# Attention outputs by features: values held in TensorE on two column halves, probabilities divided on GpSimd before their transpose

## The reference, cut to what matters

```
g = sigmoid(gates)
o_a = g[0] * softmax(q kc) vc  +  g[1] * softmax(q k_slc) v_slc  +  g[2] * softmax(q k_win) v_win
e = exp(s - m);  p = e / (sum(e) + exp(sink - m));  o_b = p v_swa
merged = sigmoid(ga) * (o_a @ w_branch_a) + sigmoid(gb) * (o_b @ w_branch_b)
h = h + merged @ w_out
```

```
x = x + concatenate([o_mla, o_dsa, o_ret]) @ w_out
x = x + square(relu(rmsnorm(x) @ w_ff1)) @ w_ff2
```

## Time and profile before

| | us |
|---|---|
| median of 3 runs | 1260.78 |
| lowest, highest | 1260.34, 1265.6 |
| time of the profiled execution | 1260.99 |
| its span in the trace | 1259.2 |

### The profile page before, as it was taken

The page is one execution under the profiler, slowest core; times in us unless marked ns, Lnnn a source line. Parts: engine busy times, 40 slices in busy tenths (PEclk is TensorE's granted clock), DMA queues, the critical chain, the costliest instruction groups (busy, mean ns, idle before and its releaser), DMA issues. The chain is left out here.

```text
span 1259.2 us, 21554 instructions
## 1 busy us (share of the span) xinstructions
PE 1228.6 (98%) x8764; PEld 1131.6 (90%) x8764; DVE 791.7 (63%) x1095; ACT 609.6 (48%) x831; POOL 66.4 (5%) x58
## 2 busy tenths in 40 slices
PE   8999999999999999999999899999999989999997
PEld 7999999989998999999999789999999978999996
DVE  4665556657866655555799655555458977654554
ACT  5444345355536443435755554444465464544343
POOL 0000000200000000000530000000004200000000
PEclk9999999999999999999999999999999999999999
DMA  9576565455335565556465056655644734566550
GB/s 286 176 227 193 175 184 149 129 159 169 134 119 199 179 192 197 173 193 185 151 126 168 28 174 203 197 175 193 187 140 119 159 101 151 174 195 192 176 198 33
DMA packets 200915, 209.62 MB, mean 166 GB/s; under 512 B 58136, under 2 KB 177552, under 8 KB 200848
## 3 DMA queue, kind: packets, MB, share of 16 engines
q1 hardware_dynamic: 200400, 208.21, 53.8%
q10 hardware_dynamic: 448, 0.46, 0.2%
HBM read 207.61 MB, written 1.05 MB: 166 GB/s over the span
## 5 line engine op out<-in xcount | busy, mean ns | idle before, releaser
L1366 DVE TENSOR_TENSOR w_lo<-raw,w_hi 128x2048 fp32r<-128x2048 f32 (+2 forms) x192 | 432.9, 2258 | 270.5 <-ACT w_hi L1014 269.9
L1014 ACT ACTIVATE w_hi<-raw 128x2048 fp32r<-128x2048 f32 (+2 forms) x192 | 359.4, 1876 | 246.3 <-PE bank L1890 214.8
L1890 PE MATMUL bank<-n_hi,w_hi 128*128 128x256 f32 (+1 forms) x1600 | 455.4, 285 | 1.5 <-DVE w_lo L1366 1.5
L1890 PE MATMUL bank<-n_hi,w_lo 128*128 128x256 f32 (+1 forms) x1600 | 452.8, 283 | 0.0
L1890 PE MATMUL bank<-n_lo,w_hi 128*128 128x256 f32 (+1 forms) x1600 | 452.7, 283 | 0.0
L1890 PEld LDWEIGHTS bank<-n_hi,w_hi 128*128 128x128 f32 (+1 forms) x1600 | 305.3, 191 | 5.6 <-DVE w_lo L1366 1.7
L1890 PEld LDWEIGHTS bank<-n_lo,w_hi 128*128 128x128 f32 (+1 forms) x1600 | 305.3, 191 | 2.1 <-issue 0.2
L1890 PEld LDWEIGHTS bank<-n_hi,w_lo 128*128 128x128 f32 (+1 forms) x1600 | 305.3, 191 | 0.0
L1890 PE MATMUL bank<-w_hi,hid_hi 128*128 128x512 f32 x440 | 172.7, 392 | 1.3 <-DVE hid_lo L1439 1.1
L1890 PE MATMUL bank<-w_lo,hid_hi 128*128 128x512 f32 x440 | 171.8, 391 | 0.0
L1890 PE MATMUL bank<-w_hi,hid_lo 128*128 128x512 f32 x440 | 171.4, 389 | 0.0
(11 more groups left out here) (268 smaller groups left out, 1485.5 us busy)
## 6 DMA issues: line engine op xcount, KB each, us to landing
raw<-in_w_ff_dram SPq DMA_DIRECT2D x64, 1024.0 KB, 5.3
raw<-in_w_in_dram SPq DMA_DIRECT2D x31, 1024.0 KB, 5.4
raw<-in_ffn_down_dram SPq DMA_DIRECT2D x22, 1024.0 KB, 4.9
raw<-in_ffn_up_dram SPq DMA_DIRECT2D x21, 1024.0 KB, 5.4
raw<-in_ffn_gate_dram SPq DMA_DIRECT2D x20, 1024.0 KB, 5.4
raw<-in_w_out_dram SPq DMA_DIRECT2D x12, 1024.0 KB, 5.1
raw<-in_w_in_dram SPq DMA_DIRECT2D x12, 256.0 KB, 4.0
raw<-in_w_uq_dram SPq DMA_DIRECT2D x24, 128.0 KB, 4.0
```

Source lines behind the costliest of these rows:

```text
L1014: nc.scalar.activation(wh(s)[:, c0:n], raw[:, s % RING, c0:n], ACT.Copy).then_inc(hi_ready, 1)
L1366: V.tensor_tensor(wl(s)[:, c0:n], raw[:, s % RING, c0:n], wh(s)[:, c0:n].bitcast(f32), ALU.subtract).then_inc(lo_ready, 1)
L1890: mm = MM(out, stat(k, a), mov(k, b), start=(first and k == 0 and n == 0), stop=(last and k == K - 1 and n == 2), skip_group_check=True)
```

## The change

Five parts:

1. **Values stationary, column halves.** `pv` holds 64 columns of values and streams the transposed probabilities of all the heads of a group (256 or 512 columns; in mla 128, since each head has its own values). The upper group writes partitions 0 to 63 of the bank, the lower group 64 to 127, so two matmuls with different columns of the array stand next to each other. The output has features on partitions.
2. **Division ahead of the turn.** A softmax sum now belongs to a column of the output, so it is divided out earlier: a new step `n` stands between `s` and `t`. VectorE makes the factor `pcoef` (reciprocal, in layer 0 times the gate), and GpSimd multiplies the round's two `probs` buffers by it in place. `t` waits on `normed` in place of `exp_done`.
3. **Branches summed in the bank.** `slc`, `win` and the compressed branch of a tile add up in one PSUM bank (step `o` `nsa`); the compressed probabilities are multiplied by their factor on VectorE (in `cs`).
4. **No output transposes** but for retention (4 in place of 16 per layer); step `o` is a copy to hi on ScalarE and a subtraction to lo on VectorE.
5. **Order.** Layer 0 starts with `swa` and ends with `win`; branch b comes before branch a. Layers 1 and 2 have a new order, in which the first quarter of `wout` (the rows of dsa and ret) stands between the mla rounds. `probsT` gets two more buffers.

```diff
-    S += gate[2] + [("cmpt", "v")] + scores[4] + weighted[2] + turned[3]
+    S += gate[2] + [("cmpt", "v")] + scores[4] + normed[3] + weighted[2] + turned[3]
...
+        scores, normed, turned, weighted = in_rounds(l, [("dsa", 0), ("dsa", 1), ("mla", 0), ("mla", 1)])
+        S += scores[0] + scores[1] + [("ukv", l)] + normed[0] + turned[0] + scores[2] + [("ukvv", l)] + normed[1] + turned[1]
+        S += [("rety", l)] + scores[3] + weighted[0] + normed[2] + weighted[1] + [("mixt", l)] + turned[2] + scores[4] + normed[3]
+        S += [("wout", l, 0)] + turned[3] + weighted[2] + normed[4] + turned[4] + weighted[3] + weighted[4]
+        S += [("wout", l, n) for n in range(1, 4)]
...
+                if st[0] == "n":
...
+                    pool.wait_ge(coef_ready, CO[(l, a, t, next(r for r in rounds(a, t) if g in r))] + 1)
+                    by = pcoef[:, RSLOT[a], t, hs].unsqueeze(2).to_broadcast([P, nh, nk])
+                    p = probs[:, q % 4, 0:nh * nk].rearrange("p (h k) -> p h k", h=nh)
+                    nc.gpsimd.tensor_tensor(p, p, by, ALU.mult).then_inc(normed, 1)
...
+                elif kind == "n":
...
+                    dve.wait_ge(exp_done, ATT[(l, a, t, r[1])] + 1)
...
+                    ins = V.reciprocal(c, sums)
+                    if a in GATE:
+                        link(ins)
+                        dve.wait_ge(*free_count(("toks", 0)))
+                        ins = V.tensor_tensor(c, c, of(gates[:, t, 8 * GATE[a]:8 * GATE[a] + 8]), ALU.mult)
+                    ins.then_inc(coef_ready, 1)
...
                 elif kind == "t":
                     q = ATT[st[1:]]
-                    pe.wait_ge(exp_done, q + 1)
+                    pe.wait_ge(normed, NRM[st[1:]] + 1)
...
-                    for i, h in enumerate(heads):
-                        for blk in range(t + 1):
-                            c = (i * (t + 1) + blk) * P
-                            mm = MM(acc[o % 2][:, h * HD:h * HD + HD], probsT[:, n % 2, c:c + P], values(a, h, blk),
-                                    start=(blk == 0), stop=(blk == t))
+                    for blk in range(t + 1):
+                        for i in range(nh if a == "mla" else 1):
+                            for rows_, heads, pT in sides:
+                                c0, n = column_of(a, heads[i]), (1 if a == "mla" else nh)
+                                mm = MM(ob[rows_, c0:c0 + n * P].rearrange("p (i c) -> p i c", c=P), values(a, heads[i], blk), pT[:, i:i + n, blk, :],
+                                        start=(first and blk == 0 and i == 0), stop=(blk == t), skip_group_check=True)
...
+                elif kind == "o":
+                    ob, ks, tok = output_blocks(st)
+                    act.wait_ge(pv_done, ON[st[1:]][1])
...
+                    nc.scalar.activation(on_hi[:, ks, tok], ob, ACT.Copy).then_inc(ot_hi, 1)
```

More of the change, by code:

```diff
@@ L138, in schedule @@
[L138 to L141, removed]
+    S += scores[0] + [("proj", 0, "nq1"), ("rope", 0, "sq1"), ("cmpt", "k")] + scores[1] + normed[0] + [("rope", 0, "nq1")] + turned[0]
@@ L142, in schedule @@
+    S += gate[6] + [("ct", 1)] + scores[8] + normed[7] + weighted[6] + [("cv", 0), ("o", 0, "nsa", 0)] + turned[7]
+    S += gate[7] + [("sigmoid",)] + normed[8] + weighted[7] + turned[8] + [("cv", 1)] + weighted[8] + [("o", 0, "nsa", 1), ("branch",)]
     S += [("wout", 0, n) for n in range(4)]
@@ L155, in schedule @@
               ("topk", l, 1, 0, 4), ("topk", l, 1, 4, 8), ("proj", l, "rg"), ("uq", l, 1),
[L156 to L165, removed]
+              ("retv", l), ("rope", l, "uq"), ("uq", l, 2), ("retn", l)]
+        scores, normed, turned, weighted = in_rounds(l, [("dsa", 0), ("dsa", 1), ("mla", 0), ("mla", 1)])
[3 more added lines that the diff above has]
+        S += [("wout", l, n) for n in range(1, 4)]
         S += [("split", 3 + 2 * l), ("root", 3 + 2 * l), ("stat", 3 + 2 * l), ("ffn2", l)]
@@ L1335, in _ @@
                 elif kind == "wout" and st[2] < 2:
[L1336 removed]
+                    ahead(SL[st], 1 if st[1] and st[2] == 0 else 2)
         @block.vector
@@ new lines, in _ @@
+                    V.tensor_tensor(on_lo[:, ks, tok], ob, on_hi[:, ks, tok].bitcast(f32), ALU.subtract).then_inc(o_free, 1)
+                elif kind == "n":
+                    _, l, a, t, g = st
+                    r = next(r for r in rounds(a, t) if g in r)
+                    if g != r[0]:
+                        continue
+                    dve.wait_ge(exp_done, ATT[(l, a, t, r[1])] + 1)
+                    hs = sorted(groups(a, t)[r[0]] + groups(a, t)[r[1]])
+                    if a in GATE:
+                        of = lambda x: x.rearrange("p (g j) -> p g j", g=2)[:, :, hs[0]:hs[len(hs) // 2 - 1] + 1]
+                    else:
+                        of = lambda x: x[:, hs[0]:hs[-1] + 1]
+                    c = of(pcoef[:, RSLOT[a], t, :])
+                    sums = of(rsum[:, RSLOT[a], t, :])
+                    if a == "swa":
+                        link(V.tensor_tensor(c, sums, of(esink[:, t, :]), ALU.add))
+                        sums = c
+                    ins = V.reciprocal(c, sums)
+                    if a in GATE:
+                        link(ins)
+                        dve.wait_ge(*free_count(("toks", 0)))
+                        ins = V.tensor_tensor(c, c, of(gates[:, t, 8 * GATE[a]:8 * GATE[a] + 8]), ALU.mult)
+                    ins.then_inc(coef_ready, 1)
+                elif kind == "wout" and st[1] and st[2] == 0:
+                    ahead(SL[st], 1)
@@ L2223, in _ @@
                     _, l, a, t, g = st
-                    heads, n, o = groups(a, t)[g], PVN[st[1:]], ON[st[1:4]][0]
+                    r = next(r for r in rounds(a, t) if g in r)
+                    if g != r[0]:
+                        continue
+                    key = output_of(l, a, t)
+                    ob, begun = acc[ON[key][0] % 2], key in opened
                     if g == 0:
```

312 lines of the change are left out of this document (143 added, 169 removed).

## The result

The changed kernel takes 1302.73 us (median of four runs), the kernel before, timed beside it, 1263.19; the ratio is 1.0306, with a 95% interval of 1.026 to 1.0352. The prediction said 1302. That median counts one run of 1796.31 us, far above the others, which the ratio leaves out: the other three took 1299.95, 1300.54 and 1304.92 us. The profiled execution took 1299.95 us, its span is 1298.2, and its mean granted clock 0.982.

What follows compares the result with a forecast made beforehand. PE, busy 98% of the span, was taken to bound the kernel. From 1261.0 us, 21 for layer 0's stalls, 10 for layers 1 and 2 and 10 for clock falls gave 1302; range 1277 to 1322.

Steps and rivals of the forecast that it cites:

- What bounds: PE, busy 98% of the span before; afterwards idle before turns, some 30 us in layer 0, 25 in layers 1 and 2.
- The chain of a round: Layer 0, scores through maxima, factor and two GpSimd products to the turn: gate at S + 6.3 us instead of S + 3.70.
- the stall is half as long: Rival: GpSimd's product with a repeated factor is quicker than the rotation's rows, or signals are shorter; 1275 us, chance 0.10.
- Layer 0: Attention's nine turns wait for GpSimd's product, whose factor stands behind the next round's maxima: 21 us longer in sum.
- Layers 1 and 2: PE waits 14.5 us per layer, against old waits, values and transposes saved: 5 us longer each, 10 for both.
- The clock: Gaps of about 2.5 us before turns drop the granted clock to half: nine falls at 1.1 us, 10 us; bounds 0 and 32.
- Part 1: Times-values on PE: column halves run side by side, halving 33.1 us of matmuls, so 16.5 us saved.
- Part 4: Output transposes on PE: 40 of 48 go, 4 us, with a 1.6 us wait before the branches' second half; 5.6 together.
- Ports: GpSimd products meeting a VectorE split would cost 1.6 us more; none expected, nothing added. Rival that they meet: 1320 to 1330, chance 0.04.
- 1239 if nothing new waited: Whole kernel: 1261 less 22 us of PE's own work, should the change bring no new waits.
- The saving of 22 us: PE's own work saved by the values matmuls (16.5 us) and output transposes with their wait (5.6 us).
- the faster case: Rival: the turn does not wait, normalized probabilities being ready before PE finishes the previous round's values; 1239 us, chance 0.06.

Runs made afterwards that it cites:

- e1_l0_factor_first: Changed kernel with, in layer 0 only, the factor step put ahead of the gate projection and next round's scores: 1273.56 us, ratio 1.0073.
- e2_factor_first: Changed kernel with the factor step put ahead of the next round's scores in all three layers: 1259.43 us, ratio 0.9972 to the kernel before.
- e4_kept_warm: Changed kernel with matmuls of zeros ahead of each turn's wait for GpSimd and the second swa scores: 1286.64 us, ratio 1.0173.
- the best: Factor-ahead order in all layers, plus in layers 1 and 2 the first mla turn ahead of dsa's two values steps: 1254.86 us, ratio 0.9937.
- e6_warm_once: Factor-ahead order in all layers, plus 13 matmuls of zeros ahead of layer 0's second swa scores: 1259.78 us, ratio 0.9972.
- three small edits: On the factor-ahead order: retention's transposes behind the first mla turn (1259.56 us), zeros before the second swa scores (1259.78), that turn ahead of dsa's values (1254.86).

## Why the prediction was right

The time was met (1302.7, or 1300.5 without the run of 1796 us, for 1302), the sign and the mechanism too: the factor's place on VectorE holds the turn, as e1_l0_factor_first and e2_factor_first show. The terms, one by one:

- **What bounds.** PE, by its waits at the turn, released by GpSimd, as written. Predicted idle there 30 + 25 us; measured 22.0 in layer 0 and 17.9 in layers 1 and 2, so the waits are a quarter shorter than forecast. A part of that is the view: it counts idle time from the end of a record, and a record lasts some 0.2 us longer than the next start needs.
- **The chain of a round.** Predicted gate at S + 6.3, measured S + 5.52. Every step up to the factor was right to 0.12 us (first maximum 1.16 for 1.17, end of the factor 2.95 for 3.07). **The term that was mis-sized is GpSimd's product:** 1.29 us was taken from the earlier trace rows, a product of two full inputs; with a factor repeated along the keys it took 1.02, so two take 2.04 for 2.6, and GpSimd is 37 us busier (103.4 for 66.4) where 45 was forecast. That was the mechanism of the rival "the stall is half as long", of which I wrote that nothing spoke for it but a missing row; it came true by a fifth, not by half.
- **Layer 0.** Predicted 21 us longer without the clock; with the clock held (e4_kept_warm) it is 17.4. From scores to scores, the first seven turns cost 1.9, 3.0, 2.2, 1.9, 3.3, 3.5 and 1.0 us for the 2.4, 3.7, 2.75, 2.6, 3.75, 4.0 and 1.7 predicted: each 0.5 to 0.7 less, of which the shorter products are 0.5. The last two together cost -0.1 for 0.2. Against these 4.4 us stand 0.7 that the sum did not have, ahead of the first turn.
- **Layers 1 and 2.** Predicted 5 each without the clock, measured 3.9 and 3.8. The shorter product is again a part of it; the rest was not taken apart. The waits stand where they were foretold, and are shorter (1.56 us before dsa's first turn for 2.0, 3.02 at the first mla round for 4.0, 2.66 at the last for 3.5). Before `ukv` PE waited 1.0 us for 1.1.
- **The clock.** Predicted nine falls at 1.1 us, 10 in all; measured 13.3 to 13.9 by e4_kept_warm, for 41 us more at 1.2 GHz than before. The price was right: 41 us are twelve times 3.4, and 13.3 / 12 is 1.1. The count was short: there were eleven stretches, and the one at 261 lasted 10.2 us, as long as three of the others. Most of them lay in the gate's matmuls and not in the turns.
- **So the sum came out by two errors of opposite sign:** stall 25 for 31, clock 14 for 10. The forecast was closer than its terms, and that is luck.
- **Part 1.** Predicted saving 16.5 us of PE; measured 14 (18.2 us for 32.0). In layer 0 of the changed kernel it lies in the stall: in the round of the earlier trace rows PE is through with the values 1.97 us before the turn can start, and the turn's start follows from the chain that begins with the scores. That is read from the timeline; no run took part 1 out by itself.
- **Part 4.** After the last turn of layer 0 the compressed values, the last values and the branches' 192 matmuls follow each other without a gap; the 1.6 us of the earlier trace rows are gone. By starts, output transposes cost 7.5 us before, with that wait, and 1.0 in e2_factor_first.
- **Ports.** Predicted that no product meets a split in this order: the longest product took 1.49 us against a median of 1.04, and none came near the 2.92 of the earlier trace rows. Right here, and no longer so once the factor is moved.
- **"1239 if nothing new waited".** The order that takes the turn's waits away gave 1259.4, the best 1254.9. The saving of 22 us was nearly a true count of PE's work (14 of values and 6.5 of transposes and their wait found), but not a time that any order here reached: what stands in its place are waits for VectorE's gate evacuation behind its weight splits, and falls of the clock. That the faster case would give 1239 was the weakest statement of the prediction.

What stays open: which part of the 16 us between 1254.9 and 1239 is VectorE's and which the clock's. In e6_warm_once, where one fall of the clock was taken away, PE waited for VectorE instead.

## What to carry to other kernels

A step that moves to another engine inherits the place of its input in that engine's order. The division was free while it stood behind the values; ahead of the turn it stood behind maxima of the next round, and a change of order alone (the factor first) was worth 41 us, where the matmuls of values saved were worth 14. Before such a change is judged, place the new producer ahead of everything that its own input does not need. And when a wait is taken away, ask the waits view for the next one: two of three small edits here only moved a wait, and the third followed from reading which.

## What the hardware showed that was not expected

- GpSimd multiplies 128x512 in place by a factor repeated over the inner dimension in 1.02 us, where two full inputs took 1.29; 128x128 took 0.38. Whether the repeated factor or the place of the output makes the difference, no run separates.
- A GpSimd product that starts 0.16 us behind a VectorE split of 2.28 us lasts 3.02 us, and the split keeps its length. A split that starts beside two running products lasts 2.87 us for 2.29.
- The granted clock fell eleven times in the 19 rounds, six of them in layer 0, where PE stands still for 1 to 3.6 us in a round and has 5.7 us of dense matmuls behind it; the first fall lasted 10.2 us, the ten others 3.4 each. With cheap matmuls of zeros in the gaps it did not fall at all inside the kernel. The Trainium skill, page TensorE: Matmul & The Clock Gate, section "HAM oscillation — how this bites in real kernels", tells of a like pattern, short bursts of matmuls and waits for DMA in turn, with a fall in each round; here there were eleven falls for 19 rounds.
- Matmuls on the two column halves run beside each other even when four records of one side are issued ahead of the other's. With sixteen they do so only in part: 32 records take 2.49 us for 1.97 at full clock.
